# Layers 2 and 3 of a four-layer transformer kernel: inputs transposed two units ahead of use, their low halves behind the next weight's low half

## The reference

```python
def second_block(x, c, norm_w, mod_w, mod_b, a_w_in, a_w_out, b_w_in, b_w_out, final_norm_w):
    slopes = alibi_slopes(N_HEADS)
    cond = jax.nn.silu(c)
    for i in range(DEPTH):
        mod = cond @ mod_w[i] + mod_b[i]
        shift, scale, gate = jnp.split(mod[:, None, :], 3, axis=-1)
        h = rms_norm(x, norm_w[i]) * (1.0 + scale) + shift
        j = i // N_MIXERS
        if i % N_MIXERS == 0:
            y = dilated_mixer(h, a_w_in[j], slopes) @ a_w_out[j]
        else:
            y = moba_mixer(h, b_w_in[j], slopes) @ b_w_out[j]
        x = x + gate * y
    return rms_norm(x, final_norm_w)
```

## Time and profile before

| | |
|---|---|
| time, median of 3 runs | 2493.15 us (2492.67 to 2493.81) |
| time of the profiled execution | 2495.73 us |
| its span, first to last instruction | 2493.9 us |
| mean granted TensorE clock | 0.995 |
| TensorE matmuls busy | 2452.6 us (98%) |
| VectorE busy | 1703.0 us (68%) |
| ScalarE busy | 1184.6 us (48%) |
| GpSimd busy | 522.9 us (21%) |
| first unit of layer 2 / of layer 3 | at 949.62 / 2002.28 us of the span |

### The profile page before, as it was taken

The page is one execution under the profiler, slowest core; times in us unless marked ns, Lnnn a source line. Parts: engine busy times, 40 slices in busy tenths (PEclk is TensorE's granted clock), DMA queues, the critical chain, the costliest instruction groups (busy, mean ns, idle before and its releaser), DMA issues.

```text
span 2493.9 us, 30840 instructions
## 1 busy us (share of the span) xinstructions
PE 2452.6 (98%) x11830; PEld 2055.0 (82%) x11830; DVE 1703.0 (68%) x2086; ACT 1184.6 (48%) x1573; POOL 522.9 (21%) x692
## 2 busy tenths in 40 slices
PE   8999999999999999999999999999999989999998
PEld 7898888888888887888888888888888878888786
DVE  5887865677787776666566666666655676667665
ACT  5557654445445544344443434444454444444543
POOL 1000000134430000533153053234300023223000
PEclk9999999999999999999999999999999999999999
DMA  7545545687767875887588677768745657777654
GB/s 237 167 136 148 149 129 188 188 269 252 250 219 242 269 260 169 271 268 253 168 257 259 202 248 242 236 210 262 252 137 181 193 176 229 226 228 228 203 193 136
DMA packets 254468, 531.80 MB, mean 213 GB/s; under 512 B 16377, under 2 KB 26945, under 8 KB 254193
## 3 DMA queue, kind: packets, MB, share of 16 engines
q1 hardware_dynamic: 253120, 526.06, 66.9%
q0 software_dynamic: 896, 3.20, 0.4%
q10 hardware_dynamic: 304, 0.57, 0.1%
HBM read 527.67 MB, written 2.10 MB: 212 GB/s over the span
## 4 chain that ended last, share of the span: by engine, by line
PE 81%; issue 11%; DVE 4%; ACT 2%; POOL 1%; DMA 0%; POOLq 0%; DVEq 0%; SPq 0%; ACTq 0%
PE proj L1020 23%; PE proj L1022 23%; PE proj L1021 23%; PE att L1070 2%; PE att L1053 2%; DVE w_lo L1697 1%; PE proj L1001 1%; ACT w_hi L1298 1%; PE att L1201 1%; PE att L1117 1%; PE proj L1006 1%; POOL slot L2001 1%; PE proj L1027 1%; PE proj L1028 1%; PE proj L1029 1%
## 5 line engine op out<-in xcount | busy, mean ns | idle before, releaser
L1697 DVE TENSOR_TENSOR w_lo<-raw,w_hi 128x1024 fp32r<-128x1024 f32 x804 | 989.8, 1235 | 579.6 <-ACT w_hi L1298 575.9
L1020 PE MATMUL proj<-w_hi,h 128*128 128x512 f32 (+1 forms) x3080 | 1227.8, 399 | 5.9 <-DVE h L1844 4.5
L1298 ACT ACTIVATE w_hi<-raw 128x1024 fp32r<-128x1024 f32 x804 | 847.6, 1057 | 767.2 <-PE proj L1022 747.4
L1022 PE MATMUL proj<-w_hi,h 128*128 128x512 f32 (+1 forms) x3080 | 1199.9, 390 | 0.0
L1021 PE MATMUL proj<-w_lo,h 128*128 128x512 f32 (+1 forms) x3080 | 1197.8, 389 | 0.0
L1020 PEld LDWEIGHTS proj<-w_hi,h 128*128 128x128 f32 x3080 | 580.2, 188 | 122.2 <-issue 9.7
L1022 PEld LDWEIGHTS proj<-w_hi,h 128*128 128x128 f32 x3080 | 579.3, 188 | 123.0
L1021 PEld LDWEIGHTS proj<-w_lo,h 128*128 128x128 f32 x3080 | 580.6, 189 | 114.0 <-issue 1.7
L2001 POOL COPY slot<-stage 32x256 f32<-32x256 f32 x640 | 481.1, 752 | 816.5 <-DVE stage L1714 781.1
L1858 DVE SCALAR_TENSOR_TENSOR mod_acc<-raw,vec,mod_acc 128x1024 f32<-128x1024 f32 x192 | 255.2, 1329 | 0.3 <-DMA raw<-in_mod_w 0.3
L1987 POOL TENSOR_TENSOR row_rstd<-row_rstd,power 128x2 f32<-128x2 f32 x5 | 3.6, 716 | 569.0 <-DVE row_rstd L1788 569.0
(11 more groups left out here) (236 smaller groups left out, 1486.2 us busy)
## 6 DMA issues: line engine op xcount, KB each, us to landing
raw<-in_a_w_in SPq DMA_DIRECT2D x320, 512.0 KB, 4.7
raw<-in_mod_w SPq DMA_DIRECT2D x192, 512.0 KB, 4.4
raw<-in_w_in_odd SPq DMA_DIRECT2D x128, 512.0 KB, 4.6
raw<-in_b_w_in SPq DMA_DIRECT2D x128, 512.0 KB, 4.3
raw<-in_w_in_even SPq DMA_DIRECT2D x100, 512.0 KB, 3.7
raw<-in_w_out_even SPq DMA_DIRECT2D x32, 512.0 KB, 4.1
raw<-in_w_out_odd SPq DMA_DIRECT2D x32, 512.0 KB, 5.4
raw<-in_a_w_out SPq DMA_DIRECT2D x32, 512.0 KB, 4.0
```

The source lines that it names most:

```text
L1020: pe.matmul(o, x_hi[:, xs], hi[:, kk, :], start=start, stop=False)
L1022: done = pe.matmul(o, x_lo[:, xs], hi[:, kk, :], start=False, stop=stop)
L1298: act.activation(m.w_hi[u.n % SPLIT_N][:, 0:size], m.raw[i][:, 0:size], ACT.Copy).then_inc(s.hi_ready, 1)
L1697: dve.tensor_tensor(m.w_lo[ring][:, 0:size], m.raw[i][:, 0:size], m.w_hi[ring][:, 0:size].bitcast(F32), ALU.subtract).then_inc(s.lo_dve, 1)
```

## The change

For layers 2 and 3:

- **Slots.** Pairs 3 to 7 get `hin` half a slot earlier, at f+p-2.5, that is ahead of unit f+p-2 instead of behind it; their `xn` moves by the same half slot. Pair 2 stays.
- **A step of its own.** The low half of pairs 2 to 7 leaves `hin` and becomes a step `hlo`, at f+p-2 (f+0.6 for pair 2). In `ORDER` it stands right behind `split`: VectorE makes it behind the low half of weight f+p+1.
- **PSUM.** For pairs 1 to 7 the next user of the bank waits for the scaled input (`val_ready`) instead of the low half.
- **Pair 0** on VectorE goes one k tile after the other: scaled input, low half, scaled input, low half, where both scaled inputs came first.
- **A new wait**: the scaled input of item n waits until n-1 pairs have their low half, since `val` has room for two.
- The view of layer 2's token order moves into a helper, `tokens_in_order`.

No instruction is added or removed.

```diff
@@ -235,7 +235,7 @@
-ORDER = ["rows", "squares", "split", "mod_start", "mod", "unit", "evac", "turn", "resid", "sum", "row", "gate", "mod_fold", "mod_cols",
+ORDER = ["rows", "squares", "split", "hlo", "mod_start", "mod", "unit", "evac", "turn", "resid", "sum", "row", "gate", "mod_fold", "mod_cols",
@@ -390,6 +390,8 @@
             slot = max(free, first - PAIRS + 2) if p < PAIRS - 2 else first + p - PAIRS + 3
+        elif layer >= 2 and p > HEAD_PAIRS:
+            slot -= 0.5
         it = plan.at(slot, "hin", layer=layer, pair=p, n=m, banks=(m % 4,), h_free=free)
...
             plan.at(boundary if p < HEAD_PAIRS else boundary + 0.2 if p == HEAD_PAIRS else slot - 1, "xn", item=it)
+        if layer >= 2 and p >= HEAD_PAIRS:
+            plan.at(slot + (0.5 if p > HEAD_PAIRS else 0.6), "hlo", item=it)
@@ -640,7 +644,10 @@
-            use(it, kind, it.banks, s.h_done, it.n + 1)
+            if it.layer >= 2 and not it.fine:
+                use(it, kind, it.banks, s.val_ready, it.ready)
+            else:
+                use(it, kind, it.banks, s.h_done, it.n + 1)
@@ -764,6 +771,12 @@
+    def tokens_in_order(self, src, out, layer):
+
+        if layer == 2:
+            return src.rearrange("p (n a) -> p a n", a=TILES), out.rearrange("p (a n) -> p a n", a=TILES)
+        return src, out
@@ -1819,29 +1832,31 @@
                 w.wait_ge(s.mod_vec_ready, 2 * (it.layer - 1))
+                w.wait_ge(s.h_done, it.n - 1)
...
-                    src = banks[j][:, part]
-                    out = val[:, j, :]
-                    if it.layer == 2:
-                        src = src.rearrange("p (n a) -> p a n", a=TILES)
-                        out = out.rearrange("p (a n) -> p a n", a=TILES)
+                    src, out = m.tokens_in_order(banks[j][:, part], val[:, j, :], it.layer)
...
                     if it.fine and j == 0:
                         done.then_inc(s.val_first, 1)
+                        w.wait_ge(s.val_first, it.layer - 1)
+                        w.wait_ge(s.h_hi_first, it.fine)
+                        dve.tensor_tensor(lo[:, 0, :], val[:, 0, :], hi[:, 0, :].bitcast(F32), ALU.subtract).then_inc(s.h_first, 1)
                 done.then_inc(s.val_ready, 1)
-                if it.fine:
-                    w.wait_ge(s.h_hi_first, it.fine)
-                    w.wait_ge(s.val_first, it.layer - 1)
-                    dve.tensor_tensor(lo[:, 0, :], val[:, 0, :], hi[:, 0, :].bitcast(F32), ALU.subtract).then_inc(s.h_first, 1)
-                rest = 1 if it.fine else 0
-                w.wait_ge(s.h_hi, it.n + 1)
-                w.wait_ge(s.val_ready, it.ready)
-                dve.tensor_tensor(lo[:, rest:, :], val[:, rest:, :], hi[:, rest:, :].bitcast(F32), ALU.subtract).then_inc(s.h_done, 1)
+                if it.pair < HEAD_PAIRS:
+                    rest = 1 if it.fine else 0
+                    w.wait_ge(s.h_hi, it.n + 1)
+                    w.wait_ge(s.val_ready, it.ready)
+                    dve.tensor_tensor(lo[:, rest:, :], val[:, rest:, :], hi[:, rest:, :].bitcast(F32), ALU.subtract).then_inc(s.h_done, 1)
+        elif kind == "hlo":
+            hi, lo = m.halves(it.n % H_RING)
+            w.wait_ge(s.h_hi, it.n + 1)
+            w.wait_ge(s.val_ready, it.ready)
+            dve.tensor_tensor(lo, m.val(it), hi.bitcast(F32), ALU.subtract).then_inc(s.h_done, 1)
```

## The result

The changed kernel takes 2500.28 us (median of 12 runs, 2497.00 to 2500.85), the kernel before 2493.60 us (12 runs beside it, 2491.93 to 2494.75). The ratio is 1.0024, 95% interval 1.0016 to 1.0032: slower, by 6.7 us in the medians (4.0 to 8.0 by the interval), where 6.1 were forecast.

A forecast was written before the change was run, and what follows sets the result against it. TensorE was busy 98%, but in two stretches a VectorE-ScalarE loop set the pace; losses of 3.59 us (layer 3) and 2.55 (layer 2) sum to 6.1, taking 2493.15 to 2499.3 us, range 2496.0 to 2502.5.

The forecast's parts named there:

- The loop: VectorE and ScalarE waiting on each other in layers 2 and 3: a turn grows from 3.78 to 4.38 us.
- Its price: Input's low half on VectorE, now ahead of the scaled input: 0.69 less 0.08 overlap, 0.61 us a turn.
- The end of a stretch: Unit f+7 starts 30.20 us after f in both layers, losing 3.59 us in layer 3, 2.55 in layer 2.
- The opening: Pair 0, one k tile after the other: first unit starts as before, both queues then 0.92 us late.
- TensorE ahead of f+4 and f+5: Sign in the trace: TensorE would idle 0.8 to 1.0 us ahead of each of these units.
- Freed PSUM: Banks released at the scaled input instead of the low half: no transposes wait for one, so zero.
- the new wait: Pair p's scaling waits for the low half of p-2, met one turn earlier on the same queue: zero.
- the loads: Weights' loads issued up to 3.6 us later; the DMA engines have room, so zero.
- TensorE sets the pace: Rival: a turn costs TensorE's 3.20 us, a gain of 6.9 us to 2486.2; chance 0.07.
- The rule of the most occupied engine: Relieving the busiest engine counts; so read, feeding TensorE earlier pays, with the sum of the gain rival, 2486.2 us.
- The clock falls: Rival: TensorE's pauses halve its clock, +1.5 to 3 us a start, 2501 to 2505 us; chance 0.09.
- Opening absorbed: Rival: the 0.92 us delay vanishes ahead of the loop, loss only 4.3 us, 2497.5; chance 0.10.

The follow-up runs named there:

- x1: Changed kernel with each low half of pairs 2 to 7 in layers 2 and 3 computed twice; 2508.56 us, ratio to before 1.0060.
- x2: Changed kernel with the low half behind the next pair's scaled input on VectorE instead of ahead of it; 2495.81 us, ratio to before 1.0010.
- x5: Kernel before with only the low half of pairs 2 to 7 moved behind the next weight's low half; 2502.44 us, ratio 1.0037.
- x7: Kernel before with only the PSUM release changed, to wait for the scaled input of pairs 1 to 7; 2492.81 us, ratio 0.9998.
- x4: Changed kernel with pairs 3 to 7's high half behind the next weight's on ScalarE, and pair 0's old order; 2487.93 us, ratio to before 0.9978.
- x8: Changed kernel with the high half of pairs 3 to 7 behind the next weight's on ScalarE, new opening kept; 2489.37 us, ratio to before 0.9982.
- x6: Kernel before with only pair 0 treated one k tile after the other, as in the changed kernel; 2494.85 us, ratio 1.0005.

## Why the prediction was right, point by point

- **What is concerned.** Two stretches of eight units; the rest kept its length within 0.1 us between them and behind; only the start of the program differed (last section). Right.
- **The loop.** 4.38 us a turn, ScalarE idle 2.00, VectorE idle 1.65 ahead of the weight's low half and not at all ahead of the input's, TensorE idle 1.38 and 1.41 ahead of f+6 and f+7: forecast 4.38, about 2.0, about 1.6, none, 1.4. x1 (twice the price, a turn 0.73 longer), x2 (out of the loop, 3.78) and x5 (alone, 4.38) show that the low half's place is the cause of the longer turn, and with it of 4.86 of the 6.11 us.
- **Its price.** 0.61 us from the low half to the scaled input, taken from overlaps in the earlier trace rows, measured 0.61 (2019.97 to 2020.58).
- **The end of a stretch.** 30.20 forecast, 30.18 and 30.19 measured; losses 2.55 and 3.59 forecast, 2.53 and 3.58 measured.
- **The opening.** 0.92 us late: pair 1's scaled input stands at 949.86 - 948.68 = 1.18 after the first unit, forecast 1.19. That this delay makes up the rest of the loss rests on the sum: the weight f+4 was to be copied 9.63 us after f and was at 9.60 in both layers (2013.37 in layer 3), with every wait on ScalarE and VectorE between them for the other of the two. No run has the changed kernel with the old opening. Two small misses. The first unit was to start as before, and starts 1.63 us after the first scaling (2002.14 to 2003.77) where it was 1.55 (2000.73 to 2002.28): 0.08 a layer. And unit f+1 was to start 5.05 us after f in layer 3 and started 6.2 after, since the whole first unit ran at half clock this time (0.50 in 2004 to 2009 above). That did not move f+7: between f and f+7 no wait of VectorE or ScalarE ended with TensorE, in either layer.
- **TensorE ahead of f+4 and f+5.** Wrong: forecast 0.8 to 1.0 us ahead of each; measured 0.43 ahead of f+4 and 0.44 ahead of f+5. Ahead of f+5 0.32 more stand before the transposes in front of the unit (2024.13), which waited for their normalised pair; their sum, 0.76, is a little under the forecast, and nearly half of it has another cause than the one named. It did not touch the forecast of the time, as f+7 comes from the loop's sum.
- **Freed PSUM, the new wait, the loads.** Zero. x7 shows it for PSUM; for the other two no trace shows a wait.
- **The rivals.** "TensorE sets the pace" did not come with this change, and came with x4: 24.8 forecast for that case in layer 2, 24.76 measured, in part because misses cancel (f+1 was 0.08 late, and the unit f+6 took 2.72 us and not 2.84); in layer 3 23.92 and not 22.6, as its first unit, with f+1 at 5.54 and not 4.10, ran longer at half clock. The rule of the most occupied engine, which the prediction cited from the Trainium skill (Perfetto Trace Analysis, Identifying the Most-Contended Engine), would, as read there, have called this change a gain; in this stretch the chain of waits decided (a turn of 4.38 us with TensorE needing 3.20), and TensorE set the pace only once the loop's turn was under TensorE's, in x4 and x8. "The clock falls" did not happen at a turn of 4.38 us; it did in x1. "Opening absorbed" holds in part with the old loop, where x6 and x7 together put it at 0.9 us behind a quick first unit and nothing behind one of 5.93; in the changed kernel the sum with the full delay fits to 0.02 us.
- **The total.** 6.1 us forecast, 6.11 in the profile's stretches, 6.7 in the medians. The difference lies within the interval of the measurement (4.0 to 8.0). How near the forecast came is partly luck: the distances before are those of one profile, with 3.74 us for layer 3's first unit, the quickest of the twenty in the table, and the prediction's own ends were 5.1 and 7.2 for other first units.

## What to carry to other kernels

Where two in-order queues hand work to each other, write down the loop (from each step to the one that it releases, back to the start) and sum it. Where that sum is larger than any engine's work in a turn, it is the pace, however idle the engines are, and a lead is used up. An instruction that fills a wait is free only in such a place: here it was paid in full each turn once it stood ahead of the next step of the loop (the changed kernel, x5), and free again behind that step (x2). To gain, cut the loop or spread it over more turns: one copy placed behind the next weight's copy took a turn from 4.38 to 3.20 us, the pace of the engine that should set it. And before two distances are compared, look whether both began at the same clock.

## What the runs showed of the hardware

**Pauses and the clock.** In the changed kernel TensorE paused for 0.43 to 1.41 us ahead of each unit from f+4 on, with the granted clock at 1.00 (2.4 GHz). In x5 it paused for 1.54 and 1.55 us once in each layer, ahead of f+2, and for 0.93 to 1.41 ahead of the later units, also at 1.00. In x1 the last pauses were 2.10 to 2.14 us, and the clock fell to half (1.2 GHz) in both layers: behind 2.10 and 2.14 us ahead of two units in a row in layer 3 (0.93 in 2038 to 2042, 0.53 in 2042 to 2045, in the rows above), and behind the first pause of 2.11 us in layer 2 (0.57 in 976 to 980). No run has repeated pauses between those of x5 and those of x1.

**The start of the program.** The runs of one kernel differ by up to 5.6 us (2489.70 to 2495.27 for the kernel before), more than most effects here. The profiles show two places where the clock differs. The kernel before, and under it x5, in 20 to 30 and in 340 to 360 us (columns as in the earlier trace rows):

```profile
20.00:30.00 10.00, 8.16 (x57) 7.92 (x56) 5.37 (x10) 4.63 (x10) 0.00 (x0) 0.83 1.00 370
340.00:360.00 20.00, 18.12 (x97) 15.35 (x96) 10.65 (x21) 11.57 (x23) 0.00 (x0) 0.91 0.33 104
```

```profile
20.00:30.00 10.00, 9.67 (x82) 9.68 (x83) 6.39 (x13) 5.22 (x9) 0.00 (x0) 1.00 1.04 369
340.00:360.00 20.00, 18.12 (x108) 15.69 (x107) 12.62 (x26) 10.83 (x22) 1.27 (x2) 1.00 0.33 107
```

Of the ten profiles eight have both dips, 0.83 and 0.91, and reach unit f of layer 2 at 947.80 to 949.62 us. Two, x5 and x8, have 1.00 in both places and reach it at 944.71 and 944.84. The dips are not all of that difference. One small transpose (out of `work_b`, at 22.61 us in the kernel before and 20.33 in x5) stands about where the first dip begins, and it already starts anywhere from 20.33 to 22.61 us. From it to unit f of layer 2 are 927.0 to 927.4 us in the eight profiles and 924.38 in both of the others. So 2.6 to 3.1 us go with the two dips, and up to 2.3 us arose ahead of them; what from, the rows don't say. Up to the opening of layer 2 the kernels do the same work in the same order, so 3 to 5 us of a single run are chance; that is why the distances inside the profiles settled what the times alone could not.
